# Index scores and the search for the 256th score moved ahead of the other input projections

## The chip, the cores and the metric

The kernel runs on one core of one Trainium2 chip. The metric is the device time of one execution in microseconds (us). Five engines work side by side: PE (TensorE, matrix products; PEld is its weight load), DVE (VectorE), ACT (ScalarE), POOL (GpSimd) and SP, which issues the transfers (DMA). Each runs its own list of instructions in order, and they wait for each other by semaphores.

## What is computed

Two layers of a decoder for a prompt of 1024 rows and a sample group of 8 x 4 rows that has 4096 cached rows each. Only the attention of layer 0 for the prompt matters here; the rest (sample attention, feed-forward layers, an RWKV-7 layer) is not edited.

```
proj = h @ w_in      # qa ka va | qb kb vb | qi ki wi  (stick-breaking | sparse | index)
oa = stick_breaking(qa, ka, va)                  # 8 heads
score = sum_h wi[h] * relu(qi[h] . ki) / sqrt(64 * 8)   # index score of every key for every query
sel = top_k(score with later keys at -inf, 256)
ob = softmax attention of qb over kb, vb, over the keys in sel only
```

qb, kb, qi and ki are turned by rotary tables (cos, sin) of their positions. The value of the 256th largest score of each query is found by a search over the bits of a float: for each of 31 bits, count the scores that are at least a candidate, and keep the bit if there are 256 or more.

## The kernel before

All rows (1024 + 32 = T = 1056) are kept transposed: features on the 128 partitions, rows along the free dimension. The stages are separated by barriers of all engines (the class Stage, its exit). Those up to the end of the prompt's attention, in order:

- `stage_enter` (L144) loads x, normalises it and transposes it to xT (in oT) and hT; SP also loads the first two weight tiles (`follow`, L174) and the page numbers, and at the end saves xT to memory (`K.x_save`).
- `stage_project` (L241) makes 24 output tiles, 12 rounds of two, of 128 features x 1056 rows each: 24 products of 128 x 128 by 352 columns per tile (L310), into two banks `acc[0]` and `acc[1]` in turn. DVE evacuates each tile: plainly in one operation (qa, ka, va, vb: L335, L337; wi: L339), or with rotary in six (qb, kb, qi, ki: L342, four of L345, L348). PE begins a tile when the bank's last content has been evacuated (semaphore `taken`) and its weights are there; SP loads weights of a tile when the product two tiles earlier is done. The rotary tables and a scratch tile lie in oT, and are loaded by SP once xT is saved. The order of the rounds is qa/ka, va/qb, vb/kb, qi/qi, ki/wi.
- `stage_rows` (L355) transposes ka, va, kb, vb, ki and wi (L372 to L378) to rows, writes the outputs, and keeps vtok (values by row) and wtok (index weights, scaled, L395).
- `stage_index_prompt` (L427): for each of the 6 query tiles that have more than 256 keys, and each of 8 index heads, PE makes the products (L445), ACT takes the relu (L456), DVE weighs and adds (L465, L468). The scores stay in `A.scores`.
- `stage_stick_prompt` (L544): 48 steps (4 head pairs, 2 query chunks of 512, 4 or 8 key tiles). Per step and two heads: PE scores (L576), ACT exp (L633), DVE cap (L654), ACT log (L635), DVE maximum (L664) and, on diagonal tiles, mask (L669), PE suffix products (L584, and L589 with the running sum that DVE makes, L682), ACT exp (L627), DVE mask on diagonal tiles (L650), PE output (L606). The score banks are three, `z[0..2]`; PE issues the suffix of step m - 2, the output of m - 3 and the scores of m in one turn. Between these, DVE carries out the search (`Threshold`, L476): 288 operations, spread evenly over the turns by the line quoted below. One operation is a count over one query tile (L500, with an accumulator read of its own), or one of three small ones per bit (L524, L532, L535).
- `stage_sparse_prompt` (L691) uses scores and thresholds for the masked softmax attention.

```
goal = Threshold.OPS * (2 * m + 1) // (2 * M + 6)
while asked < goal:
    search.advance(dve, A, asked)
    asked += 1
```

Of the kernel before, what the change touches and what calls it, by code (L numbers as in the profile page):

```python
# [21 lines left out]
P = 128  # L22
# [81 lines left out]
def row3(ap):  # L104

    return ap.rearrange("p (c n) -> p c n", c=NCH)
# [134 lines left out]
def stage_project(nc, K, w_in, hT, A, free, w):  # L241

    W = w_in[0].rearrange("(k p) n -> p k n", p=P)
    with Stage(nc, "proj") as s:
        s.sems.append(K.saved)
        cos, sin, half = (free[:, i, :] for i in range(3))
        acc = [s.ps(f"acc{u}", [P, NCH, 512]) for u in range(2)]
        w_loaded = [s.sem(f"w_loaded{u}") for u in range(2)]
        tables, product, taken, steps = s.sem("tables"), s.sem("product"), s.sem("taken"), s.sem("steps")
        block = s.block()  # L250

        DHS = bass.ds

        def pair_src(i, base):
            return [(W[:, :, DHS(i * P + base, P)], slice(0, P))]

        def qb_src(i):
            return [(W[:, :, DHS(i * DH + OFF_QB, DH)], slice(0, DH)),
                    (W[:, :, DHS(i * DH + OFF_QB + HP * DH, DH)], slice(DH, P))]

        ki = [(W[:, :, OFF_KI:OFF_KI + DH], slice(0, DH)), (W[:, :, OFF_KI:OFF_KI + DH], slice(DH, P))]
        wi = [(W[:, :, OFF_WI:OFF_WI + 8], slice(0, 8))]
        rounds = [
            (4, lambda i: pair_src(i, 0), "query", lambda i: A.qa[:, DHS(i, 1), :],
             lambda i: pair_src(i, OFF_KA), "copy", lambda i: A.ka[:, DHS(i, 1), :]),
            (4, lambda i: pair_src(i, OFF_VA), "copy", lambda i: A.va[:, DHS(i, 1), :],
             qb_src, "rope", lambda i: A.qb[:, DHS(i, 1), :]),
            (1, lambda i: pair_src(0, OFF_VB), "copy", lambda i: A.vb[:, :, :],
             lambda i: pair_src(0, OFF_KB), "rope", lambda i: A.kb[:, :, :]),
            (2, lambda i: pair_src(2 * i, OFF_QI), "rope", lambda i: A.qi[:, DHS(2 * i, 1), :],  # L270
             lambda i: pair_src(2 * i + 1, OFF_QI), "rope", lambda i: A.qi[:, DHS(2 * i + 1, 1), :]),
            (1, lambda i: ki, "rope", lambda i: A.ki[:, :, :],
             lambda i: wi, "weights", lambda i: A.wi[:, :]),
        ]
        n_loads = [[len(r[1 + 3 * u](0)) for u in range(2)] for r in rounds]

        @block.sync
        def _(sp):
            sp.sem_inc(w_loaded[0], 16)
            sp.sem_inc(w_loaded[1], 16)  # L280
            with sp.Fori(0, rounds[0][0] - 1) as i:
                for u in range(2):
                    sp.wait_ge(product, 2 * i + u + 3)
                    for src, cols in rounds[0][1 + 3 * u](i + 1):
                        sp.dma_start(w[u][:, :, cols], src).then_inc(w_loaded[u], 16)
            sp.wait_ge(K.saved, 16)
            sp.dma_start(cos[:, :], K.cos).then_inc(tables, 16)
            sp.dma_start(sin[:, :], K.sin).then_inc(tables, 16)
            done = rounds[0][0]
            for n, r in enumerate(rounds[1:]):  # L290
                with sp.Fori(0, r[0]) as i:
# [4 lines left out]
                done += r[0]  # L296

        @block.tensor
        def _(pe):
            pe.sem_inc(product, 2)  # L300
            done, loads = 0, [0, 0]
            for n, r in enumerate(rounds):
                with pe.Fori(0, r[0]) as i:
                    for u in range(2):
                        pe.wait_ge(w_loaded[u], 16 * (i * n_loads[n][u] + n_loads[n][u] + loads[u]))
                        pe.wait_ge(taken, 2 * i + 2 * done + u + 1)
# [7 lines left out]
                loads = [loads[u] + r[0] * n_loads[n][u] for u in range(2)]  # L314

        @block.vector
        def _(dve):
            dve.sem_inc(taken, 2)  # L318
            link = Link(dve, steps)
            done = 0  # L320
            for n, r in enumerate(rounds):
                if n == 1:
                    dve.wait_ge(tables, 32)
                per = sum({"rope": 2}.get(r[2 + 3 * u], 0) for u in range(2))
                with dve.Fori(0, r[0]) as i:
                    if per:
                        link.enter(i, per)
                    for u in range(2):
                        kind, dst = r[2 + 3 * u], r[3 + 3 * u](i)
                        dve.wait_ge(product, 2 * i + 2 * done + u + 3)  # L330
# [9 lines left out]
                        else:  # L340
# [9 lines left out]
                if per:  # L350
                    link.leave(r[0], per)
                done += r[0]


def stage_rows(nc, K, A, O):  # L355


    with Stage(nc, "rows") as s:
# [6 lines left out]
        def _(pe):  # L365
            for t in range(NT + 1):
# [10 lines left out]
                pe.transpose(tp[t % 2][0:n, 2, 2 * P:2 * P + DH], A.ki[0:DH, 0, cols], K.ident[0:DH, 0:DH])  # L377
                pe.transpose(tp[t % 2][0:n, 2, 320:328], A.wi[:, cols], K.ident[0:8, 0:8]).then_inc(turned, 1)  # L378

        @block.vector  # L380
        def _(dve):
            for t in range(NT + 1):
# [6 lines left out]
                dve.tensor_copy(row[t % 2][0:n, 2, 0:328], tp[t % 2][0:n, 2, 0:328]).then_inc(taken, 1)  # L389
                dve.wait_ge(taken, 3 * t + 3)  # L390
                if t < NT:
                    dve.tensor_copy(A.vtok[:, t, 0:512], row[t % 2][:, 1, :])
                    dve.tensor_copy(A.vtok[:, t, 512:640], row[t % 2][:, 2, P:2 * P])
# [33 lines left out]
def stage_index_prompt(nc, K, A):  # L427

    units = [(qt, h) for qt in CHOOSING for h in range(8)]
    with Stage(nc, "index") as s:  # L430
        kept = [s.sb(f"kept{i}", [P, SEQ]) for i in range(3)]
        prod = [s.ps(f"prod{i}", [P, 1024]) for i in range(3)]
        product, relued, weighed = s.sem("product"), s.sem("relued"), s.sem("weighed")
        block = s.block()

        @block.tensor
        def _(pe):
            for u, (qt, h) in enumerate(units):
                if u >= 3:
                    pe.wait_ge(relued, u - 2)  # L440
                rows = slice((h % 2) * DH, (h % 2) * DH + DH)
# [17 lines left out]
        def _(dve):  # L459
            for u, (qt, h) in enumerate(units):  # L460
# [15 lines left out]
class Threshold:  # L476
# [5 lines left out]
    def __init__(self, s):  # L482
        self.n = len(CHOOSING)
        self.found, self.flip, self.cand, self.more = (s.sb(x, [P, self.n], I32) for x in ("found", "flip", "cand", "more"))
        self.count = s.sb("count", [P, self.n])
        self.junk = s.sb("junk", [P, sum((qt + 1) * P for qt in CHOOSING)], BF16)
# [57 lines left out]
def stage_stick_prompt(nc, K, A, oT):  # L544
# [12 lines left out]
    with Stage(nc, "stick") as s:  # L557
        expd, soft, wgt = (s.sb(x, [P, R, 2, 512]) for x in ("expd", "softplus", "weight"))
        later = s.sb("later", [P, 2, 2, 512])
        search = Threshold(s)  # L560
# [82 lines left out]
        def _(dve):  # L643
            asked = 0
            for m in range(M + 3):
# [2789 lines left out]
```

## Time and profile before

| | us |
|---|---|
| time, median of 3 executions (lowest to highest) | 5399.53 (5394.25 to 5403.45) |
| time of the profiled execution | 5401.57 |
| its span, first to last instruction | 5399.8 |
| PE busy | 4599.8 (85%) |
| DVE busy | 2292.2 (42%) |
| ACT busy | 1088.0 (20%) |
| POOL busy | 350.0 (6%) |
| mean granted clock of PE, as a share of full speed | 0.914 |

Busy time is the union of an engine's recorded instructions. PE's products are pipelined and their ends are modelled, so a busy PE need not be one at its peak. The granted clock is 1.00 at 2.4 GHz and 0.50 at 1.2 GHz; a mean in between is a mix of the two. In lists of instructions a row has start, duration, engine, line, operation, tiles, shapes, how many were merged, and in brackets the idle time of the engine in front of it with what ended it. In groups a row has the engine, line and shapes, how many, then the busy time in us and the mean in ns of one, then the idle time before them.

### The profile page before, as it was taken

To read this page: it belongs to the slowest core of one execution; us is meant where nothing else is said; L and a number is where in the kernel's file an instruction comes from. 1 tells how busy PE (TensorE), PEld (TensorE's weight loads), DVE (VectorE), ACT (ScalarE), POOL (GpSimd) and SP (SyncE) were. 2 spreads that over 40 slices of the span, in tenths; PEclk is the share of its full clock that TensorE was granted. 3 is DMA by queue.
4 is the path that set the end of the run, shared out by engine and by line. 5 is a ranking of instruction groups with operands and counts; after the bars stand their busy time and mean duration, and the time that the engine had idled before them with its cause. 6 is when DMAs were issued, how large, how long until landed. Compare 5 with 4: busy or idle time off the path is not lost. (4 is left out here: it accounts for less than half of the span.)

```text
span 5399.8 us, 75557 instructions
## 1 busy us (share of the span) xinstructions
PE 4599.8 (85%) x30371; PEld 2899.1 (54%) x30371; DVE 2292.2 (42%) x3248; ACT 1088.0 (20%) x1971; POOL 350.0 (6%) x523
## 2 busy tenths in 40 slices
PE   8997777777767799999996999577777879999997
PEld 5663223344434466665663645376765546666564
DVE  1248997369921323232004122487685242323102
ACT  1004333344431122221000010222122022222000
POOL 0000000410063000000000000111110000000000
PEclk9998987889978899999997989788888889999998
DMA  2110000289964011111101221412213201111111
GB/s 92 47 39 27 1 0 1 52 288 352 357 181 139 24 35 39 35 39 47 33 22 58 71 82 61 164 30 53 57 30 142 63 24 39 35 39 46 35 33 43
DMA packets 434190, 398.60 MB, mean 74 GB/s; under 512 B 71613, under 2 KB 351717, under 8 KB 429494
## 3 DMA queue, kind: packets, MB, share of 16 engines
q1 hardware_dynamic: 419042, 347.23, 20.2%
q0 software_dynamic: 12288, 21.00, 1.4%
q10 hardware_dynamic: 2584, 26.50, 1.3%
q8 instruction: 197, 3.23, 0.3%
q14 instruction: 79, 0.65, 0.0%
HBM read 341.43 MB, written 53.06 MB: 73 GB/s over the span
## 5 line engine op out<-in xcount | busy, mean ns | idle before, releaser
L2086 PE MATMUL fup_acc<-h,w_up_first 128*128 128x352 f32 x2112 | 636.8, 462 | 28.1 <-ACTq L2093 28.1
L2086 PE MATMUL fup_acc<-h,fup_w 128*128 128x352 f32 x2112 | 632.0, 459 | 0.0
L2086 PEld LDWEIGHTS fup_acc<-h,w_up_first 128*128 128x128 f32 x2112 | 403.5, 191 | 255.4 <-ACTq L2093 30.2
L2086 PEld LDWEIGHTS fup_acc<-h,fup_w 128*128 128x128 f32 x2112 | 401.3, 190 | 223.5
L2129 DVE TENSOR_SCALAR fup_c<-fup_u,taps 128x1072 f32<-128x1072 f32 x88 | 73.7, 838 | 852.1 <-ACT last_u L2106 852.1
L310 PE MATMUL proj_acc<-hT,w_in 128*128 128x352 f32 (+1 forms) x1152 | 344.0, 462 | 1.8 <-DVEq L318 1.8
L1970 PE MATMUL fdown_acc<-hidden,w_down_first 128*128 128x352 f32 x1056 | 317.4, 463 | 0.0
L1970 PE MATMUL fdown_acc<-hidden,fdown_w 128*128 128x352 f32 x1056 | 314.5, 460 | 2.4 <-DVE h L1889 2.4
L310 PEld LDWEIGHTS proj_acc<-hT,w_in 128*128 128x128 f32 (+1 forms) x1152 | 215.4, 187 | 129.9 <-issue 12.4
L1970 PEld LDWEIGHTS fdown_acc<-hidden,w_down_first 128*128 128x128 f32 x1056 | 202.1, 192 | 115.7 <-issue 6.5
L2099 ACT ACTIVATE fup_u<-fup_acc 128x704 f32<-128x704 f32 x88 | 66.7, 757 | 974.6 <-PE fup_acc L2086 974.6
L1970 PEld LDWEIGHTS fdown_acc<-hidden,fdown_w 128*128 128x128 f32 x1056 | 200.0, 190 | 116.5 <-issue 3.4
L2016 DVE COPY h<-fdown_acc 128x1056 f32<-128x1056 f32 x16 | 20.1, 1255 | 541.0 <-PE fdown_acc L1970 541.0
L500 DVE TENSOR_SCALAR_CACHE_REDUCE stick_junk<-scores,stick_cand 128x384 bf16<-128x384 f32 (+1 forms) x186 | 167.2, 941 | 0.7
L2624 POOL TENSOR_TENSOR scan_om<-scan_low,scan_level 128x512 f32<-128x512 f32 x80 | 122.8, 1546 | 508.4 <-PE scan_u L2706 389.3
L584 PE MATMUL stick_z<-stick_softplus,tri 128*128 128x512 f32 (+3 forms) x192 | 93.3, 617 | 65.6 <-DVE stick_softplus L669 44.5
L1995 ACT ACTIVATE fdown_square<-h 128x1056 f32<-128x1056 f32 x16 | 17.3, 1083 | 652.1 <-DVE h L2016 652.1
L1190 DVE MAX8 sstick_best<-vtok 32x8 f32<-32x4100 f32 x32 | 141.1, 4409 | 0.0
L1193 DVE MATCH_REPLACE8 vtok<-sstick_best,vtok 32x4100 f32<-32x4100 f32 x32 | 140.8, 4401 | 0.0
L2706 PE MATMUL scan_u<-scan_Tm,scan_om 64*64 64x64 f32 x2560 | 95.4, 234 | 42.8 <-DVE scan_TT L3031 35.4
L2713 PE MATMUL scan_u<-scan_X,scan_TT 64*64 64x64 f32 x2048 | 86.6, 242 | 49.7 <-ACT scan_X L2902 43.7
L1103 ACT ACTIVATE sstick_kT<-sstick_tp 128x512 f32<-128x512 f32 x248 | 127.8, 596 | 2.4 <-PE sstick_tp L996 2.3
(582 smaller groups left out, 6846.5 us busy)
## 6 DMA issues: line engine op xcount, KB each, us to landing
sstick_own<-in_cache_sb_k SPq DMA_DIRECT2D x128, 256.0 KB, 5.8
qb<-in_cache_sb_k SPq DMA_DIRECT2D x128, 256.0 KB, 6.2
qi<-in_cache_sb_v SPq DMA_DIRECT2D x128, 256.0 KB, 5.8
ka<-in_cache_sb_v SPq DMA_DIRECT2D x128, 256.0 KB, 6.2
w_up_first<-in_ffn_w_up SPq DMA_DIRECT2D x44, 512.0 KB, 3.7
fup_w<-in_ffn_w_up SPq DMA_DIRECT2D x44, 512.0 KB, 3.8
w_down_first<-in_ffn_w_down SPq DMA_DIRECT2D x8, 1408.0 KB, 7.0
fdown_w<-in_ffn_w_down SPq DMA_DIRECT2D x8, 1408.0 KB, 7.0
```

The costliest lines, as they stand in the source:

```text
L310: last = pe.matmul(acc[u][0:m, c, 0:CW], w[u][:, k, 0:m], hT[:, k, c * CW:(c + 1) * CW], start=(k == 0), stop=(k == KD - 1))
L500: self.mark(dve.tensor_scalar(self.junk[:, at:at + (CHOOSING[t] + 1) * P], score, at_least, 0.0, ALU.is_ge, ALU.add, accum_out=self.count[ ...
L584: last = pe.matmul(z[m % R][:, par, c:512], K.tri[:, :], soft[:, m % R, par, c:512], start=False, stop=True, skip_group_check=True)
L1103: act.activation(kT[:, p % 2, :, i % 4, (i // 4) * P:(i // 4 + 1) * P], tp[t % 3][:, :].rearrange("p (f n) -> p f n", f=HP), ACT.Copy).the ...
L1190: link(dve.max(best[:, :], score))
L1193: link(dve.match_replace(score, best[:, :], score, LOW))
L1970: last = pe.matmul(acc[n % 2][:, c, 0:CW], w[n % 2][:, k, :], src[:, k, c * CW:(c + 1) * CW], start=(k == 0), stop=(k == kt - 1))
L2086: last = pe.matmul(acc[u][:, c, 0:CW], w[u][:, k, :], hT[:, k, c * CW:(c + 1) * CW], start=(k == 0), stop=(k == KD - 1))
L2129: link(dve.tensor_scalar(c, ubuf[u][:, 0:CO], tap[0], tap[3], ALU.mult, ALU.add))
L2624: pool.tensor_tensor(om[:, heads(g), :], low2[:, heads(g), 0, :], level[:, l, :].unsqueeze(1).to_broadcast(full), ALU.mult).then_inc(om_re ...
L2706: last = pe.matmul(spot(h, c, False), om[half(c), h, :], Tm[half(c), h, :], start=True, stop=True, skip_group_check=True)
L2713: last = pe.matmul(spot(h, c, False), TT[half(c), h, :], X[half(c), h, :], start=True, stop=True, skip_group_check=True)
```

## The change

The 24 tiles are projected in two stages: first the six of the index (qi, ki, wi), then the other 18. The index stage runs between the two. The search is taken out of `stage_stick_prompt` and put into the second projection stage, where DVE does a share of it after each evacuation, by weights of 2 for a rotary tile and 4 for another. The index stage transposes wi itself, in place of `stage_rows`, and SP loads the first two weight tiles of the other projections there. The rotary tables are loaded in `stage_enter`, into vtok. Loops of `stage_project` are written out. Scratch tiles are laid into tensors that are idle at the time, and `A.scores` lives until the end of the attention, where two tiles of the sample stages are laid into it.

```diff
+def input_rounds(W, A):
...
+    index = [
+        (2, lambda i: pair_src(2 * i, OFF_QI), "rope", lambda i: A.qi[:, DHS(2 * i, 1), :],
+         lambda i: pair_src(2 * i + 1, OFF_QI), "rope", lambda i: A.qi[:, DHS(2 * i + 1, 1), :]),
+        (1, lambda i: ki, "rope", lambda i: A.ki[:, :, :],
+         lambda i: wi, "weights", lambda i: A.wi[:, :]),
+    ]
+    others = [
+        (4, lambda i: pair_src(i, 0), "query", lambda i: A.qa[:, DHS(i, 1), :],
+         lambda i: pair_src(i, OFF_KA), "copy", lambda i: A.ka[:, DHS(i, 1), :]),
+        (4, lambda i: pair_src(i, OFF_VA), "copy", lambda i: A.va[:, DHS(i, 1), :],
+         qb_src, "rope", lambda i: A.qb[:, DHS(i, 1), :]),
+        (1, lambda i: pair_src(0, OFF_VB), "copy", lambda i: A.vb[:, :, :],
+         lambda i: pair_src(0, OFF_KB), "rope", lambda i: A.kb[:, :, :]),
+    ]
+    return index, others
...
+def stage_project(nc, K, name, rounds, hT, A, w, done_too=None, junk=None):
...
+        cos, sin, half = K.tables
...
+        search = Threshold(s, junk) if junk is not None else None
...
         def _(sp):
...
+                for i in range(1 if n == 0 else 0, r[0]):
                     for u in range(2):
-                        sp.wait_ge(product, 2 * i + 2 * done + u + 1)
+                        sp.wait_ge(product, 2 * (done + i) + u - 1)
                         for src, cols in r[1 + 3 * u](i):
                             sp.dma_start(w[u][:, :, cols], src).then_inc(w_loaded[u], 16)
                 done += r[0]
+            if done_too is not None:
+                sp.wait_ge(done_too, 16)
...
         def _(dve):
...
+            kinds = [r[2 + 3 * u] for r in rounds for i in range(r[0]) for u in range(2)]
+            room = [2 if kind == "rope" else 4 for kind in kinds]
...
                             link(last)
+                            dve.sem_inc(taken, 1)
                             link(dve.tensor_tensor(dst, dst, row3(half[:, :]), ALU.add))
-                            dve.sem_inc(taken, 1)
...
+                        if search:
+                            goal = Threshold.OPS * sum(room[:at + 1]) // sum(room)
+                            while asked < goal:
+                                search.advance(dve, A, asked)
+                                asked += 1
                 done += r[0]
+            if search:
+                assert asked == Threshold.OPS
+                search.finish(dve, A.least[:, :])
...
-                pe.transpose(tp[t % 2][0:n, 2, 320:328], A.wi[:, cols], K.ident[0:8, 0:8]).then_inc(turned, 1)
...
-                dve.tensor_scalar(A.wtok[0:n, t, :], row[t % 2][0:n, 2, 320:328], (DH * 8) ** -0.5, None,
-                                  ALU.mult).then_inc(stepped, 1)
...
+def stage_index_prompt(nc, K, A, free, follow):
...
+        def _(sp):
+            for dst_w, dram in follow:
+                sp.dma_start(dst_w, dram).then_inc(followed, 16)
+            sp.wait_ge(followed, 16 * len(follow))
...
         def _(pe):
+            for t in range(NT + 1):
+                n = P if t < NT else NS
+                last = pe.transpose(prod[2][0:n, t * 8:t * 8 + 8], A.wi[:, t * P:t * P + n], K.ident[0:8, 0:8])
+            last.then_inc(turned, 1)
...
         def _(dve):
+            dve.wait_ge(turned, 1)
+            for n, ts in ((P, slice(0, NT)), (NS, slice(NT, NT + 1))):
+                dve.tensor_scalar(A.wtok[0:n, ts, :], prod[2][0:n, 0:8 * NT + 8].rearrange("p (t h) -> p t h", h=8)[:, ts, :],
+                                  (DH * 8) ** -0.5, None, ALU.mult).then_inc(laid, 1)
+            dve.wait_ge(laid, 2)
...
-                goal = Threshold.OPS * (2 * m + 1) // (2 * M + 6)
-                while asked < goal:
-                    search.advance(dve, A, asked)
-                    asked += 1
...
-                goal = Threshold.OPS * (2 * m + 2) // (2 * M + 6)
-                while asked < goal:
-                    search.advance(dve, A, asked)
-                    asked += 1
-            assert asked == Threshold.OPS
-            search.finish(dve, A.least[:, :])
...
                     stage_enter(nc, K, I.x_prompt, I.x_sample, I.page_table, I.norm_mix_pre[0], oT, hT, A,
-                                [(w[0][:, :, :], W[:, :, 0:P]), (w[1][:, :, :], W[:, :, OFF_KA:OFF_KA + P])])
-                    stage_project(nc, K, I.att_w_in, hT, A, oT, w)
+                                [(w[0], W[:, :, OFF_QI:OFF_QI + P]), (w[1], W[:, :, OFF_QI + P:OFF_QI + 2 * P]),
+                                 (K.tables[0], K.cos), (K.tables[1], K.sin)])
+                    stage_project(nc, K, "proji", index, hT, A, w, done_too=K.saved)
+                    stage_index_prompt(nc, K, A, free, [(w_later[0], W[:, :, 0:P]), (w_later[1], W[:, :, OFF_KA:OFF_KA + P])])
+                    stage_project(nc, K, "proj", others, hT, A, w_later, junk=oT[:, 0:2, :].rearrange("p k t -> p (k t)").bitcast(BF16)[:, 0:A.scores.shape[1]])
                 stage_rows(nc, K, A, O)
```

## Rows read from the trace of the kernel before

**Rows 1.** Stretches of time: projection, rows, index, stick-breaking. Stretch: length, busy by engine, clock, DMA, GB/s
```profile
46.60:391.90 345.30, 344.04 (x1152) 215.43 (x1152) 92.88 (x74) 0.00 (x0) 0.00 (x0) 0.99 0.15 40
391.90:423.30 31.40, 19.81 (x108) 15.81 (x108) 20.46 (x53) 0.00 (x0) 0.00 (x0) 0.69 0.54 181
423.30:475.60 52.30, 46.68 (x160) 24.18 (x160) 44.78 (x54) 35.99 (x48) 0.00 (x0) 0.92 0.00 1
475.60:806.00 330.40, 243.90 (x746) 98.62 (x746) 308.42 (x706) 121.83 (x154) 0.00 (x0) 0.89 0.00 1
```

**Rows 2.** Groups of instructions of the search, first 1000 us
```profile
L500 DVE TENSOR_SCALAR_CACHE_REDUCE stick_junk<-scores,stick_cand 128x384 bf16<-128x384 f32 (+1 forms) x186 | 167.2, 941 | 0.7
...
L500 DVE DVE_READ_ACCUMULATOR stick_junk<-scores,stick_cand 128x1 f32 x186 | 15.4, 83 | 0.0
...
L524 DVE SCALAR_TENSOR_TENSOR stick_cand<-stick_found,stick_flip 128x6 int32<-128x6 int32 x31 | 5.0, 163 | 0.7
```

**Rows 3.** Waits of the stick-breaking stage: total us, times, longest
```profile
ACT stick_expd L635 <- DVE stick_expd L654: 159.9, 48, 5.7
...
PE stick_z L584 <- DVE stick_softplus L669: 44.5, 27, 3.1
```

**Rows 4.** Order of time, stick-breaking stage: PE's products of steps with 512 columns
```profile
657.28 1.98 PE L584 MATMUL stick_z<-stick_softplus,tri 128*128 128x512 f32 x4 [1.91 <-DVE stick_softplus L669]
...
659.10 1.88 PE L589 MATMUL stick_z<-stick_later,negones 128*128 128x512 f32 x4
...
664.50 1.08 PE L606 MATMUL stick_o<-stick_weight,vtok 128*64 128x512 f32 x4 [0.52 <-DVE stick_weight L650]
...
672.61 1.13 PE L576 MATMUL stick_z<-qa,ka 64*128 64x512 f32 x4
```

**Rows 5.** Order of time, same stage: DVE and ACT in a step of 384 columns
```profile
671.77 0.42 DVE L650 TENSOR_TENSOR stick_weight<-stick_weight,bound 128x256 f32<-128x256 f32 x1
...
672.70 0.93 ACT L635 ACTIVATE stick_expd<-stick_expd,one 128x768 f32<-128x768 f32 x1 [5.41 <-DVE stick_expd L654]
...
673.66 0.95 DVE L664 TENSOR_TENSOR stick_softplus<-stick_expd,stick_z 128x768 f32<-128x768 f32 x1 [0.52 <-ACT stick_expd L635]
...
675.27 0.89 DVE L682 TENSOR_TENSOR stick_later<-stick_softplus,stick_later 128x768 f32<-128x768 f32 x1
```

**Rows 6.** Stretches of 2 us around the same step
```profile
670.00:672.00 2.00, 0.11 (x1) 0.00 (x0) 2.00 (x5) 0.00 (x0) 0.00 (x0) 1.00 0.00 0
...
676.00:678.00 2.00, 2.00 (x5) 1.09 (x4) 2.00 (x6) 0.00 (x0) 0.00 (x0) 0.50 0.00 0
```

**Rows 7.** The projection's tile: ns least/median/most of one, first and last start, forms
```profile
L310 PE MATMUL proj_acc<-hT,w_in x1152: 459/459/951, 46.6 to 390.2; 128*128 128x352 f32 x184, 128*8 128x352 f32 x8
L345 DVE TENSOR_TENSOR oT<-proj_acc,oT x40: 1246/1252/1262, 193.1 to 381.4; 32x1056 f32<-32x1056 f32 x40
L335 DVE TENSOR_SCALAR qa<-proj_acc x4: 1258/1258/1258, 64.1 to 149.3; 128x1056 f32 x4
L337 DVE COPY ka<-proj_acc x4: 1258/1258/1258, 78.3 to 163.5; 128x1056 f32 x4
...
L339 DVE COPY wi<-proj_acc x1: 1245/1245/1245, 390.7 to 390.7; 8x1056 f32<-8x1056 f32 x1
```

**Rows 8.** Order of time, stick-breaking stage: a count of the search and what follows
```profile
598.15 1.27 DVE L500 TENSOR_SCALAR_CACHE_REDUCE stick_junk<-scores,stick_cand 128x1024 bf16<-128x1024 f32 x1
599.35 0.08 DVE L500 DVE_READ_ACCUMULATOR stick_junk<-scores,stick_cand 128x1 f32 x1
599.47 0.17 DVE L532 TENSOR_SCALAR stick_more<-stick_count 128x6 int32<-128x6 f32 x1
```

**Rows 9.** Groups of the rows stage; last, a transfer: KB, us to landing
```profile
L378 PE MATMUL rows_tp<-ident,wi 8*128 8x8 f32 (+1 forms) x9 | 2.2, 239 | 0.0
...
L395 DVE TENSOR_SCALAR wtok<-rows_row 128x8 f32<-128x8 f32 (+1 forms) x9 | 1.5, 164 | 0.0
...
x_save<-oT SPq DMA_DIRECT2D x1, 4224.0 KB, 11.4
```

More of the change, by code:

```diff
@@ L238, in _, with pair_src, qb_src @@
             take(NT)
[L241 to L246, printed above, removed]
+def input_rounds(W, A):
+    DHS = bass.ds
+    def pair_src(i, base):
+        return [(W[:, :, DHS(i * P + base, P)], slice(0, P))]
+    def qb_src(i):
+        return [(W[:, :, DHS(i * DH + OFF_QB, DH)], slice(0, DH)),
+                (W[:, :, DHS(i * DH + OFF_QB + HP * DH, DH)], slice(DH, P))]
+    ki = [(W[:, :, OFF_KI:OFF_KI + DH], slice(0, DH)), (W[:, :, OFF_KI:OFF_KI + DH], slice(DH, P))]
+    wi = [(W[:, :, OFF_WI:OFF_WI + 8], slice(0, 8))]
+    index = [
[13 more added lines that the diff above has]
+    return index, others
@@ L250, in stage_project @@
         block = s.block()
[L252 to L274, printed above, removed]
@@ L280, in _ @@
             sp.sem_inc(w_loaded[1], 16)
[L281 to L291, printed above, removed]
+            done = 0
+            for n, r in enumerate(rounds):
+                for i in range(1 if n == 0 else 0, r[0]):
                     for u in range(2):
-                        sp.wait_ge(product, 2 * i + 2 * done + u + 1)
+                        sp.wait_ge(product, 2 * (done + i) + u - 1)
                         for src, cols in r[1 + 3 * u](i):
@@ L296, in _ @@
                 done += r[0]
+            if done_too is not None:
+                sp.wait_ge(done_too, 16)
         @block.tensor
         def _(pe):
-            pe.sem_inc(product, 2)
             done, loads = 0, [0, 0]
             for n, r in enumerate(rounds):
-                with pe.Fori(0, r[0]) as i:
+                for i in range(r[0]):
                     for u in range(2):
-                        pe.wait_ge(w_loaded[u], 16 * (i * n_loads[n][u] + n_loads[n][u] + loads[u]))
-                        pe.wait_ge(taken, 2 * i + 2 * done + u + 1)
+                        loads[u] += n_loads[n][u]
+                        pe.wait_ge(w_loaded[u], 16 * loads[u])
+                        if done + i >= 1:
+                            pe.wait_ge(taken, 2 * (done + i) + u - 1)
                         m = 8 if r[2 + 3 * u] == "weights" else P
@@ L313, in _ @@
                 done += r[0]
-                loads = [loads[u] + r[0] * n_loads[n][u] for u in range(2)]
         @block.vector
         def _(dve):
-            dve.sem_inc(taken, 2)
             link = Link(dve, steps)
-            done = 0
+            kinds = [r[2 + 3 * u] for r in rounds for i in range(r[0]) for u in range(2)]
+            room = [2 if kind == "rope" else 4 for kind in kinds]
+            asked = done = 0
             for n, r in enumerate(rounds):
[L322 to L327, printed above, removed]
+                for i in range(r[0]):
                     for u in range(2):
+                        at = 2 * (done + i) + u
                         kind, dst = r[2 + 3 * u], r[3 + 3 * u](i)
-                        dve.wait_ge(product, 2 * i + 2 * done + u + 3)
+                        dve.wait_ge(product, at + 1)
                         if kind != "weights":
@@ L3347, in build @@
             A.vtok = sb(att, "vtok", [P, NT, 640])
+            A.scores = sb(att, "scores", [P, sum((qt + 1) * P for qt in CHOOSING)])
+            spare = A.vtok[:, :, :].rearrange("p t n -> p (t n)")
+            K.tables = [spare[:, i * T:(i + 1) * T] for i in range(3)]
             with ExitStack() as c:
```

43 lines of the change are left out of this document (22 added, 21 removed).

## Prediction

> **What bounds the kernel now.** I read the busy time of each engine stage by stage first, then the groups of instructions of the stage that has the search, then its waits, and at last single steps in order of time. The stages are separated by barriers, so what an edit is worth is read stage by stage. In the table of stages the reader is to see which engine is full in each [rows 1]: the input projections keep TensorE (PE) at 344.0 of 345.3 us with VectorE (DVE) at 92.9; in the index stage DVE, at 44.8 of 52.3, sets the pace, with ACT close; in the stick-breaking stage DVE is busy for 308.4 of 330.4 us while PE has 243.9 and a granted clock of 0.89. So the search sits in the one stage of this stretch in which DVE is already the bound, and DVE idles for 250 us in a stage that PE bounds.
>
> The groups say how much of the 308 us is the search [rows 2]: 186 counting passes of 167.2 us, their 186 accumulator reads of 15.4, and three small instructions per bit, 31 of each, of which one group has 5.0. With the other two small groups at the same 0.16 us and the six counts of the sign pass (6 x about 0.95) it is 167 + 15 + 15 + 6 = 204 us as recorded. DVE's own work for attention is the rest, about 105 us net of overlap. The waits show who pays [rows 3]: ACT's logarithm waits for DVE's cap 48 times, 159.9 us in all, and PE's suffix product waits another 44.5 us for DVE.
>
> **The change, part by part.**
>
> *The search leaves the stick-breaking stage.* What ends last there afterwards? PE per full step (512 columns, no half clock): the two products of the suffix, 1.82 us from start to start and 1.88, the output 1.08 and the scores 1.13 [rows 4]; end to end that is 5.9, and since the last two overlap their successors I take 5.6. There are 24 such steps of 48. A narrow diagonal step is bounded by the round between DVE and ACT instead: mask of the weights at 671.77, cap, logarithm at 672.70, maximum at 673.66, mask, the sum from 675.27 for 0.89 [rows 5]; what the search has in between lies under the logarithm, so a step of 384 columns costs 4.3 to 4.4. Four of the operations in this round scale with the width, each by 0.25 to 0.3 us per 128 columns (0.89 for three such blocks of two heads), so about 1 us less for each block: 3.4 at 256 columns, 2.5 at 128 (estimates), 8 steps each. Sum: 24 x 5.6 + 8 x (4.35 + 3.4 + 2.5) = 134 + 82 = 216. The first step has to pass through the round before PE has a second product, and the last one through the round, the suffix and the output; I put 10 for both: 226 at full clock. The clock takes some of it: after 2 us with PE at 0.11 busy it stands at 0.50 (1.2 GHz) while PE is at 2.00 of 2.00 [rows 6]. A mean of 0.89 is 22% of the stage at half clock; those gaps of PE come in part from DVE's lateness, which goes, and in part from the narrow steps, which stay. Keeping all 22% with PE always the bound would give 226 / 0.89 = 254; I take 240. The stage falls from 330 to 240: **-90 us**; the bounds are -104 (full clock) and -65 (265: 254 and 11 us of waits that I cannot see here).
>
> *The search goes between the evacuations of 18 projected tiles.* A tile of 128 columns is ready every 14.2 us (four evacuations of qa from 64.1 to 149.3, two tiles each) [rows 7]. DVE's room: the change deals 288 operations out by weights, 4 for a plain evacuation and 2 for a rotary one, 62 in all, so 18.6 or 9.3 operations per tile. A bit is nine operations. From one count's start to the next is its length less 0.07 (598.15 to 599.35 for the recorded 1.27) [rows 8], so the six counts of a bit take 167.2 / 31 - 6 x 0.07 = 5.0, the last read and the three small ones with their waits about 0.9: 5.9 us, 0.65 per operation, some 189 us in all. A plain tile needs 1.26 + 12.2 = 13.4 us, a rotary tile 1.26 + 4 x 1.25 + 1.26 + 6.1 = 13.6 [rows 7]. Both are under 14.2, the evacuation comes before the search, and PE needs a bank only one tile later: PE does not wait, and 17 of the 18 shares cost nothing, covered by PE's 14.2 us a tile. If the cover fails, each us that DVE needs above 14.2 costs up to 18. The last tile's share has no cover: rotary evacuation 7.5 + 10 operations 6.5 + the finish 0.3 = 14.3 us after PE's last product, where before one evacuation of 1.25 stood [rows 7]: **+13**.
>
> The recorded lengths and the spacing of counts speak differently here. The Trainium skill ("VectorE: DVE Perf Modes", The DRAIN you can't avoid) says that the next operation cannot issue until the pipe of the one in front is empty. Laid end to end by that rule, the search is 204 us, a plain tile 14.4, and the sum would be some 5 us later; the rows, where the next count starts before the recorded end of the one in front, speak for the spacing.
>
> *Two projection stages in place of one, with the index stage between.* The first tile of a stage costs 17.5 us from PE's start at 46.6 to 64.1, not 14.2, since PE starts at half clock [rows 7, 6]; PE is idle for some 5 us at the end of the index stage, so this is paid twice: **+3**. One barrier more: **+1** (bounds 0.7, the step from DVE's last index operation into the next stage, to 2). SP's queue: the two tables go ahead of the page numbers and the saving of x in the loading stage, and nobody there waits for either; the save lands 11.4 us after its issue [rows 9], inside the 89 us of the six index tiles, so SP's new wait at their end is over long before. The two first weight loads of the other projections are issued at the start of the index stage, where SP has nothing else: no cost. The later weight loads keep their one-tile lead.
>
> *Index weights turned in the index stage.* Nine transposes of about 0.24 us and nine scalings of 0.16 [rows 9] leave the rows stage (**-1**); the same transposes and two scalings precede the index products (+2, of which about 1 comes back because PE is no longer at half clock there): **+1**. Loops written out, buffers laid into other tensors, the sample stages' new places: 0, bounds -2 to +2; PE's loop cost shows in no row (1.8 us idle in the whole stage).
>
> **The sum.** -90 + 13 + 3 + 1 - 1 + 1 = **-73 us** against the profiled execution's 5401.6 us (span 5399.8): 5328.6. That execution lies 2.0 above the median of the runs shown, 5399.5, so I say 5327. Nothing downstream moves: the sparse stage needs scores and thresholds, which are both there earlier.
>
> **Rivals.**
> (a) *Another wait takes the place of DVE's.* Stick-breaking stays a chain over three engines with three banks; if each step still ends with PE waiting for the round of rows 5, full steps too, the stage would come to 285 or more: a full step is then 4.4 x 1024/768 + two masks, about 6.7, and the clock stays at 0.89: (24 x 6.7 + 82 + 10) / 0.89 = 284. Gain of 46 instead of 90: 5371. For it: the two-step lead of the suffix leaves under 1 us of slack in a full step by my count. Against it: full steps off the diagonal have no mask, and their work on DVE is three operations, a little over 3 us of 5.6.
> (b) *The search is not hidden.* DVE at 14.4 or more per tile makes it the bound: at the recorded lengths +5, with 0.3 us more for each count 192 x 0.3 = 58 us, less the 14 us of slack that 18 tiles hold: +44. That gives 5332 to 5371. For it: only 0.6 to 0.8 us are free per tile. Against it: the same counts were measured beside a busy PE in the stick-breaking stage.
> (c) *PE's clock collapses in the stick-breaking stage, and the kernel gets slower.* The mechanism is that of rows 6: a PE that pauses at the narrow steps falls to 1.2 GHz, and the PE-bound steps that now set the time run at that speed. At half clock throughout, a full step is 11.2, a 384-column step 7.7, then 5.1 and 2.6: 24 x 11.2 + 8 x 15.4 + 20 = 412 us, 82 more than now: 5499. It decides once the stage exceeds 313 us, that is when some 174 of them are at half clock (mean 0.72). The stage has 0.89 with more pauses than it will have; the rows stage, at 0.69, shows such a mean is possible [rows 1]. The Trainium skill ("TensorE: Matmul & The Clock Gate", HAM oscillation) describes this: pauses between bursts send the engine back to the lower clock again and again. The trace agrees on the fall, not on its lasting.
>
> **How the numbers follow.** Forecast 80%, its own range 5305 to 5358: -104 + 18 less 8 for index, rows and barriers at their lower ends, to -65 with +24. (a) 10%, (b) 7%, (c) 3%. The range 5305 to 5362 holds most of the forecast (0.72) and the lower half of (b) and a little of (a): 0.8. A measurement of this kernel cannot tell less than about 0.2% (11 us) from no change. Faster: forecast, (a) and nearly all of (b), 95%; same: what is left of (b), 2%; slower: (c), 3%.
>
> **What would show it.** In the changed profile: no count under the stick-breaking stage, which should last 226 to 265 us with PE rather than DVE the fullest engine, and ACT's 159.9 us of waiting for the cap down to a third; evacuations in the second projection stage still 14.2 us apart; 12 to 16 us between PE's last projection product and the rows stage; the index stage within 2 us of 52.3. Wrong would be: tile spacing above 14.5 (then b), full steps at 6.5 or more with PE waiting for DVE or ACT (a), a granted clock under 0.75 in the stage (c).

## The result, and the profile after

The changed kernel took 5314.37 us (median of 4 executions, 5305.44 to 5318.03), the kernel before beside it 5400.68 (4 executions, 5394.25 to 5403.45): a ratio of 0.9839, 95% interval 0.9822 to 0.9856, or 86 us less. The forecast was 73 less. The profiled execution took 5318.03 us with a span of 5316.4.

The stages first, with the columns of [rows 1]: the stretch and its length, busy time by engine, the granted clock, the DMA share and GB/s. In order they are the index projection, the index stage, the second projection with the search, the rows stage and stick-breaking. The last line is a small stage late in the kernel, needed only at the end.

```profile
46.10:135.90 89.80, 88.19 (x288) 51.13 (x288) 38.90 (x31) 0.00 (x0) 0.00 (x0) 0.97 0.14 42
135.90:189.30 53.40, 47.07 (x169) 25.27 (x169) 45.07 (x56) 35.87 (x48) 0.00 (x0) 0.89 0.08 20
189.30:462.70 273.40, 258.37 (x864) 165.43 (x864) 238.72 (x524) 0.00 (x0) 0.00 (x0) 0.97 0.12 31
462.70:492.00 29.30, 18.25 (x99) 14.86 (x99) 19.68 (x43) 0.00 (x0) 0.00 (x0) 0.73 0.58 195
492.00:724.00 232.00, 215.52 (x744) 88.48 (x744) 133.29 (x224) 125.29 (x153) 0.00 (x0) 0.98 0.00 1
...
3055.00:3091.00 36.00, 31.50 (x104) 16.65 (x104) 14.37 (x26) 12.69 (x11) 0.00 (x0) 0.95 0.32 132
```

Against [rows 1]: projection 345.3 to 89.8 + 273.4, which is 17.9 more; index 1.1 more; rows 2.1 less; stick-breaking 330.4 to 232.0, 98.4 less. Together that is 81.5 less. The sparse stage begins its first product at 724.3 in place of 805.9, 81.6 earlier. From there to the end it is 4592.1 us, 4593.9 before. DVE's busy time says what moved: 308.4 to 133.3 in stick-breaking, while the second projection has 238.7. PE, with 215.5 of 232.0, is now the fullest engine of stick-breaking, and its idle time there is 16.5 us, 86.5 before.

The waits of the stick-breaking stage (engine, line and the engine waited for; us in total, times, the longest):

```profile
DVE stick_softplus L675 <- ACT stick_expd L651: 48.1, 48, 1.2
ACT stick_expd L651 <- DVE stick_expd L669: 46.1, 48, 1.6
...
PE stick_z L600 <- DVE stick_softplus L680: 14.6, 23, 1.8
```

The second line answers to the 159.9 us of [rows 3], the third to the 44.5. ACT waited 3.3 us for each cap, because DVE was in a count when the exponential was done; now it is 1.0.

The evacuations of the second projection (ns least/median/most of one, first and last start, forms):

```profile
L334 DVE TENSOR_SCALAR qa<-proj_acc x4: 1258/1258/1258, 206.7 to 291.9; 128x1056 f32<-128x1056 f32 x4
...
L341 DVE TENSOR_TENSOR kb<-proj_acc,vtok x1: 1258/1258/1258, 448.1 to 448.1; 128x1056 f32<-128x1056 f32 x1
```

The first tile's evacuation starts at 206.7 and the eighteenth's at 448.1, and 206.7 + 17 x 14.2 = 448.1: no tile is late. What DVE waits for PE's products in this stage,

```profile
DVE qa L334 <- PE proj_acc L313: 19.7, 4, 17.7
...
DVE ka L336 <- PE proj_acc L313: 4.3, 4, 1.7
```

with four smaller lines for the other tiles, is 29.0 us in all. Less the 17.7 for the first tile, that is 11.3 over 17 tiles: 0.7 us of room per tile, and the forecast had 0.6 to 0.8. No line has PE waiting for DVE. The end of the stage in order of time (start, duration, engine, line, operation, tiles, shapes, how many):

```profile
448.14 1.26 DVE L341 TENSOR_TENSOR kb<-proj_acc,vtok 128x1056 f32<-128x1056 f32 x1 [1.21 <-PE proj_acc L313]
...
455.91 0.17 DVE L552 TENSOR_TENSOR proj_found<-proj_found,proj_more 128x6 int32<-128x6 int32 x1
...
462.04 0.17 DVE L556 TENSOR_TENSOR least<-proj_found,proj_flip 128x6 int32<-128x6 int32 x1
463.16 1.09 PE L377 MATMUL rows_tp<-ident,ka 128*128 128x128 f32 x4 [15.05 <-PEq L95]
```

This is the cost of the new place: the rotary evacuation until 455.9, then ten operations of the search and its finish until 462.2, which no product covers, and PE idle for 15.05 us.

### The profile page after: what moved, and what is told of

It reads as the page before. It is cut to its first block and busy times, and to the rows that moved or that the text cites. A ratio compares the mean times of both kernels' runs of the same rounds, so it can differ in the third digit from the quotient of the medians.

```text
span 5316.4 us, 75362 instructions
## 1 busy us (share of the span) xinstructions
PE 4564.2 (86%) x30371; PEld 2890.8 (54%) x30371; DVE 2301.2 (43%) x3241; ACT 1093.0 (21%) x1971; POOL 351.0 (7%) x523
## 5 line engine op out<-in xcount | busy, mean ns | idle before, releaser
L313 PE MATMUL proj_acc<-hT,oT 128*128 128x352 f32 x864 | 258.4, 462 | 6.2 <-SPq L287 6.2
L313 PEld LDWEIGHTS proj_acc<-hT,oT 128*128 128x128 f32 x864 | 165.4, 192 | 99.4 <-SPq L287 7.1
L517 DVE TENSOR_SCALAR_CACHE_REDUCE oT<-scores,proj_cand 128x384 bf16<-128x384 f32 (+1 forms) x186 | 164.4, 942 | 1.1
L2135 DVE SCALAR_TENSOR_TENSOR fup_c<-fup_u,taps,fup_c 128x1072 f32<-128x1072 f32 x88 | 117.4, 1335 | 12.8 <-DVE fup_c L2134 0.3
```

The source lines that it names most:

```text
L313: last = pe.matmul(acc[u][0:m, c, 0:CW], w[u][:, k, 0:m], hT[:, k, c * CW:(c + 1) * CW], start=(k == 0), stop=(k == KD - 1))
L517: self.mark(dve.tensor_scalar(self.junk[:, at:at + (CHOOSING[t] + 1) * P], score, at_least, 0.0, ALU.is_ge, ALU.add, accum_out=self.count[ ...
L2135: link(dve.scalar_tensor_tensor(out=c, in0=ubuf[u][:, 1:1 + CO], scalar=tap[1], in1=c, op0=ALU.mult, op1=ALU.add))
```

## The experiments

Theory: the search cost its time because it stood in a stage bound by DVE's rounds, and costs nothing beside PE's tiles, the last tile excepted. Rivals: the new order of the stages brings the gain by itself; or the search still costs time where it is now; or the number of DVE's operations matters and not their place. An execution's time from the sparse stage on varies (last section), so the stage lengths and the place of the sparse stage's first product (724.3 and, again, 723.3 for the changed kernel) are read beside the times. Diffs are against the changed kernel, unless said otherwise.

**The search put back between the stick-breaking steps, in the new order of the stages.**

```diff
+                goal = Threshold.OPS * (2 * m + 1) // (2 * M + 6)
+                while asked < goal:
+                    search.advance(dve, A, asked)
+                    asked += 1
...
-                    stage_project(nc, K, "proj", others, hT, A, w_later, junk=...)
+                    stage_project(nc, K, "proj", others, hT, A, w_later)
```

> The new order of the stages is kept, the search goes back between the steps of stick-breaking. Theory (the gain is the search's place, the new order only costs): stick-breaking back at 325 to 335 us with DVE at about 308 and a clock near 0.89, the second projection stage 7.5 us of rotary evacuation after PE's last product instead of 14; the kernel 5 to 12 us slower than before (one more start at half clock 3, one more barrier 1, the tail 6). Rival (the new order itself brings part of the gain, by the clock or the earlier weight loads): 20 us or more faster than before with the search back in its old place.

5428.83 us (10 executions), ratio to the kernel before 1.0047 (1.0031 to 1.0063). Second projection and stick-breaking, columns as above, then the wait for the cap:

```profile
189.30:456.00 266.70, 258.12 (x864) 165.31 (x864) 54.02 (x43) 0.00 (x0) 0.00 (x0) 0.98 0.12 32
486.00:815.00 329.00, 248.68 (x736) 101.43 (x744) 308.71 (x705) 122.45 (x153) 0.00 (x0) 0.86 0.00 0
```

```profile
ACT stick_expd L652 <- DVE stick_expd L671: 153.3, 48, 5.7
```

With the search the 308.7 us of DVE, the 329 us of the stage and the 153 us of waits are all back. The sparse stage begins at 815.3, 9.4 later than before: that is what the new order costs, together with the small edits that came with it, so it brings nothing by itself. The median is 30 above that of the kernel before beside it (5398.55), where 5 to 12 had been expected and the stages account for 9.4; the last group of experiments comes back to this.

**The search left out.**

```diff
+            dve.memset(A.least[:, :], 0.0)
...
-                    stage_project(nc, K, "proj", others, hT, A, w_later, junk=...)
+                    stage_project(nc, K, "proj", others, hT, A, w_later)
```

> The search is left out; the thresholds are set to 0. Theory (the search is hidden under PE but for the share of the last tile): the projection stage shorter by 6.5 to 8 us, all of it after PE's last product, stick-breaking unchanged at 232, the kernel 5 to 10 us faster than the changed one (5304 to 5310). Rival (the counts slow PE or the evacuations): the spacing of the tiles falls below what the changed kernel shows and the kernel is 20 us or more faster than the changed one.

5318.14 us, ratio 0.9841 (0.981 to 0.9872). Second projection and stick-breaking:

```profile
188.40:455.10 266.70, 258.31 (x864) 165.38 (x864) 54.04 (x44) 0.00 (x0) 0.00 (x0) 0.98 0.12 32
484.50:716.00 231.50, 214.06 (x736) 88.29 (x744) 133.28 (x224) 125.19 (x153) 0.00 (x0) 0.98 0.00 1
```

184.7 us of DVE's work gone (238.7 less 54.0) shorten the stage by 6.7: that is the uncovered share of the last tile, and all that the search still costs in this stage. The sparse stage begins at 716.3, 7 to 8 earlier. The time expected, 5304 to 5310, did not come: the gain is lost in what executions differ by.

**The widest count made twice per bit**, to see where the cover ends.

```diff
+            if at == self.n:
+                self.mark(dve.tensor_scalar(self.junk2, index_scores(A, CHOOSING[at - 1]), self.cand[:, at - 1:at].bitcast(F32), 0.0,
+                                            ALU.is_ge, ALU.add, accum_out=self.again[:, :]))
```

> The count over the 1024 scores is made twice for each of the 31 bits: 31 x 1.2 = 37 us more on DVE in the second projection stage. Theory (DVE has 11 us left in the stage, its waits for PE after the first tile): the stage grows by 37 - 11 = 26 us (22 to 30) and DVE's waits for PE vanish; kernel 5336 to 5344. Rival 1 (DVE has much room): 0 to 8 us. Rival 2 (DVE is the bound already): 35 to 40.

5365.46 us (10 executions), ratio 0.9939 (0.9917 to 0.996). The stage, then a wait that the changed kernel does not have:

```profile
190.90:490.40 299.50, 264.03 (x864) 167.50 (x864) 274.86 (x586) 0.00 (x0) 0.00 (x0) 0.94 0.11 29
```

```profile
PE proj_acc L315 <- DVEq L349: 9.9, 4, 5.1
```

36.1 us more on DVE, less the 11.3 of room, are 24.8; the stage grew by 26.1, and PE now waits until a bank is evacuated, and for 25.64 us in place of 15.05 at the end of the stage. The search fitted by 0.7 us per tile, and rival (b) was that close. The sparse stage begins at 751.5, 27 later than in the changed kernel; the median lies 51 above it, where 5336 to 5344 had been expected, and no stage before the sparse one holds the rest.

**Equal shares**, 16 operations after each tile, rotary or not.

```diff
-            room = [2 if kind == "rope" else 4 for kind in kinds]
+            room = [1 for kind in kinds]
```

> The changed kernel with the search dealt out in equal shares, 16 operations per tile, in place of 18.6 beside a plain and 9.3 beside a rotary evacuation. A plain tile then takes DVE 11.7 us and a rotary one 18.0, above the 14.2 of PE. Theory (DVE falls behind at each rotary tile and what it is late by shows after PE's last product): 2 to 3 us late and a longer last share, the projection stage 280 us (278 to 283) in place of 273. Rival (only the sum over the stage counts): 273 within 1.

5330.18 us (one execution). The stage:

```profile
188.70:472.90 284.20, 258.27 (x864) 165.30 (x864) 238.37 (x524) 0.00 (x0) 0.00 (x0) 0.95 0.12 30
```

10.8 us longer with the same work, a little more than the 278 to 283 expected. The evacuation of kb, the last tile, starts at 453.40, which is 5.9 later than in the changed kernel if counted from the stage's first product, and PE is then idle for 26.04 us, not 15.05. The weights of 2 and 4 are what keeps rotary tiles on time.

**A plain tile last, with no share.** The last round projects kb before vb, and vb's tile gets no search.

```diff
+            room[-1] = 0
```

> The last two tiles change places, so that a plain evacuation is last, and the last tile gets no share of the search; the other 17 get it all. Theory (the 14 us after PE's last product are the last tile's own evacuation and share): 1.3 us of evacuation and what DVE is late by then, 1 to 4 us, are left; the kernel 9 to 12 us faster than the changed one. Rival (DVE has no room for it in the 17 tiles): the same work ends later inside the stage, the gain is under 5 us.

5324.64 us (5293.34 to 5354.58), ratio 0.9862 (0.9801 to 0.9924). The stage:

```profile
188.40:451.00 262.60, 258.39 (x864) 165.42 (x864) 237.56 (x524) 0.00 (x0) 0.00 (x0) 0.99 0.13 33
```

10.8 us shorter, as expected: the tail was the last tile's. The sparse stage begins at 712.9, 11.4 earlier, but the executions lie 61 us apart, and their time does not show a gain.

**The same, and 18 of the 288 operations left for stick-breaking, one per full-width step, right behind the cap.**

```diff
+LEFT = 18
...
+                    if c == 0 and asked < Threshold.OPS:
+                        search.advance(dve, A, asked)
+                        asked += 1
...
```

> As the run with a plain evacuation last and no share for the last tile, and besides the last 18 of the 288 operations of the search (two bits) are done in stick-breaking, one in each of the first 18 full steps, under the logarithm. Theory: DVE is no longer late at the end of the projections, the stage 260 to 262 us (13 under the changed kernel), stick-breaking 232 to 235, with one more barrier of 1 us: 9 to 13 us faster than the changed kernel beside it. Rival (an operation of the search in a step costs its length there): stick-breaking 245 or more, no gain over the changed kernel.

5319.21 us (5306.8 to 5341.5), ratio 0.9855 (0.9829 to 0.9881). Projection and stick-breaking:

```profile
188.40:449.30 260.90, 258.29 (x864) 165.60 (x864) 226.87 (x493) 0.00 (x0) 0.00 (x0) 0.99 0.13 33
479.20:711.00 231.80, 214.64 (x744) 87.99 (x744) 144.30 (x255) 125.22 (x153) 0.00 (x0) 0.98 0.00 1
```

11.0 us of DVE's work cost stick-breaking nothing there, and the sparse stage begins at 711.1. Still no gain in the median.

**A useless count of 1.2 us in each stick-breaking step, behind the cap or at the end of the step.** Two kernels with the same three lines at two places; the first stands between cap and maximum, while ACT makes the logarithm.

```diff
+                    if m >= 1:
+                        dve.wait_ge(dosed, m)
+                    dve.tensor_scalar(junk[:, :], index_scores(A, NT - 1), 0.0, 0.0, ALU.is_ge, ALU.add, accum_out=tally[:, :]).then_inc(dosed, 1)
```

> The changed kernel, and in each of the 48 steps of stick-breaking one count over 1024 scores of no use (1.2 us, 58 in all on DVE), placed between the cap and the maximum, where DVE waits for ACT's logarithm. Theory (the place in the round between DVE and ACT decides): free in full steps, where the logarithm takes 1.15 us, 0.3 to 0.7 us in each narrow one: the stage 232 + 12 (8 to 16). Rival (only the sum of DVE's work counts: 133 + 58 is still under PE's 215): 0 to 3.

> The same count, placed at the end of each step, behind the running sum. Theory: it lies in the round of the 24 narrow steps with its whole 1.2 us (29) and in part in the 8 full diagonal steps (6), and is free in the 16 full steps off the diagonal, which have over 1 us to spare: the stage 232 + 35 (28 to 42). Rival (only the sum counts): 0 to 3.

The stage with the count behind the cap (5338.36 us, one execution):

```profile
491.70:726.20 234.50, 215.41 (x744) 88.33 (x744) 185.66 (x320) 125.33 (x153) 0.00 (x0) 0.98 0.00 1
```

The stage with the count at the end of the step (5342.2, one execution):

```profile
493.00:748.50 255.50, 221.82 (x744) 90.26 (x744) 186.11 (x320) 122.05 (x153) 0.00 (x0) 0.96 0.00 1
```

The count is 58 us of DVE's work in both (58.2 and 58.0), DVE's busy time differs by 0.5 us, and the stage by 21: 2.5 us longer in the one, 23.5 in the other. Behind the cap the result misses the expected 8 to 16. In the changed kernel DVE's maximum waits there for the logarithm (in brackets the idle time, at 256, 384 and 512 columns):

```profile
572.30 0.69 DVE L675 TENSOR_TENSOR stick_softplus<-stick_expd,stick_z 128x512 f32<-128x512 f32 x1 [0.79 <-ACT stick_expd L651]
...
576.07 0.95 DVE L675 TENSOR_TENSOR stick_softplus<-stick_expd,stick_z 128x768 f32<-128x768 f32 x1 [1.00 <-ACT stick_expd L651]
...
580.71 1.22 DVE L675 TENSOR_TENSOR stick_softplus<-stick_expd,stick_z 128x1024 f32<-128x1024 f32 x1 [1.22 <-ACT stick_expd L651]
```

So nearly the whole count fits: with it the suffix of a 256-column step comes 0.26 us later behind that of the 128-column step (3.42 in place of 3.16), and those of wider steps by 0.05 at most. At the end of the step the expected 28 to 42 was too much as well: 23.5. ACT's wait for the cap, 46.1 us in the changed kernel, is 98.7 there:

```profile
ACT stick_expd L653 <- DVE stick_expd L671: 98.7, 48, 3.5
```

Place decides, not the amount.

**The scores issued ahead of the output on PE.**

```diff
+                if m < M:
+                    scores(m)
                 if m >= 3:
                     output(m - 3)
-                if m < M:
-                    scores(m)
```

> The changed kernel; in each turn of stick-breaking PE issues the scores of step m ahead of the output of step m - 3, so that the exponential of step m can begin 0.4 to 1 us earlier. Theory (in the narrow steps the round of cap, logarithm, maximum, masks and sum on DVE and ACT sets the pace, and in full steps PE's own work; the scores are there in time for both): the stage stays within 3 us of 232. Rival (the loop through PE, suffix, output, scores and then the round, sets the pace in the narrow steps): 24 narrow steps shorter by 0.2 to 0.5 us, the stage 220 to 227.

5312.76 us (5305.65 to 5319.76), ratio 0.9834 (0.9818 to 0.985). The stage:

```profile
488.50:716.00 227.50, 216.13 (x744) 88.42 (x744) 132.95 (x224) 122.87 (x153) 0.00 (x0) 0.98 0.00 1
```

My expectation failed: from the first product of stick-breaking to that of the sparse stage it is 226.8 us, 231.7 in the changed kernel. The rival had the size (220 to 227), but not where it comes from, since only one of the three narrow intervals shrinks:

```profile
565.76 0.71 PE L600 MATMUL stick_z<-stick_softplus,tri 128*128 128x128 f32 x4
...
568.40 1.13 PE L600 MATMUL stick_z<-stick_softplus,tri 128*128 128x256 f32 x4
...
572.45 1.56 PE L600 MATMUL stick_z<-stick_softplus,tri 128*128 128x384 f32 x4 [0.30 <-DVE stick_softplus L680]
```

The suffix of a 256-column step now follows that of the 128-column step after 2.50 to 2.65 us, in place of 3.16, in seven of the eight pairs (not in the first), and PE no longer waits for it. That is 4.1 of the 4.9; most of the rest lies in the first round of narrow steps. The two intervals behind it stay as in the changed kernel (3.96 to 4.05 and 4.91). So PE's own order set the first of the narrow steps, and the round over DVE and ACT the other two.

**The same kernels again, and the kernel before with 15 us of useless additions at the end of its index stage.** The last one's diff, against the kernel before:

```diff
+            for n in range(12):
+                dve.wait_ge(weighed, len(units) + n)
+                dve.tensor_tensor(kept[0][:, :], kept[1][:, :], kept[2][:, :], ALU.add).then_inc(weighed, 1)
```

> The changed kernel once more, beside those that follow. Theory (what differs between executions of one program lies behind the attention, where stages come out at one clock or the other): the stages up to the sparse attention within 2 us of the first profile (273 and 232 us), the time 5305 to 5325, ratio 0.982 to 0.987.

> The kernel before once more, for a second profile. Theory (the part of the kernel from the sparse attention on varies from one execution to the next, whichever program): the stages up to there as in the first profile within 2 us (stick-breaking 330), the rest between 4588 and 4611 us, the band of the programs run so far. Rival (the rest is fixed for this program): 4594 within 2.

> The kernel before, with 12 additions of no use by VectorE at the end of the index stage, about 15.5 us in which TensorE has nothing to do; everything behind begins that much later. Theory (a shift alone moves the later stages to the other clock or not by chance): the rest of the kernel in the band 4588 to 4611, spread of the times 20 us or more, median 5408 to 5430. Rival (the rest does not care when it begins): median 5414 to 5418, spread under 10.

The changed kernel again: 5319.91 us (5304.75 to 5333.76), ratio 0.9833 (0.9812 to 0.9855), second projection 273.5. The kernel before again: 5402.6, its sparse stage beginning at 806.4, the rest 4594.5. That is the rival's number: the two profiles of the kernel before agree from the sparse stage on, so they show no variation, though among its executions beside other experiments there are 5419 and 5425. Delayed: 5426.17 (5411.95 to 5442.17), ratio 1.0048 (1.0035 to 1.0062). Its additions, in order of time:

```profile
475.90 15.08 DVE L476 TENSOR_TENSOR index_kept<-index_kept 128x1024 f32<-128x1024 f32 x12
```

They put the sparse stage 11.8 us later, not 15: from its first product to that of the sparse stage, stick-breaking took 326.1 us, 329.7 and 329.8 in the two profiles of the kernel before. Yet the median stands 24 above the kernel before beside it (5402.07); it and the spread of 30 us are those expected, not the rival's. So a shift alone, with no step of any later stage edited, changes what later stages take, and the 30 us of the first experiment need no cause in the order of the stages itself. That they have none there is not shown.

## Why the prediction was right

The mechanism was the forecast's, and the size differs by the stick-breaking term. Two of the prediction's readings do not hold as put, and neither changes a term. PE is busy for 46.7 us of the index stage, more than DVE's 44.8 [rows 1], so busy time alone does not show that DVE sets the pace there; and PE's idle time in the whole projection stage is 1.3 us, not 1.8.

*The search leaves the stick-breaking stage*: forecast -90, measured -98.4. Two parts were mis-sized, in opposite directions, and that they cancel in part is luck. The products of PE in order of time, at the start of one round of narrow steps:

```profile
570.34 0.71 PE L600 MATMUL stick_z<-stick_softplus,tri 128*128 128x128 f32 x4
...
573.50 1.13 PE L600 MATMUL stick_z<-stick_softplus,tri 128*128 128x256 f32 x4 [0.60 <-DVE stick_softplus L680]
...
577.54 1.56 PE L600 MATMUL stick_z<-stick_softplus,tri 128*128 128x384 f32 x4 [0.40 <-DVE stick_softplus L680]
...
582.45 1.99 PE L600 MATMUL stick_z<-stick_softplus,tri 128*128 128x512 f32 x4 [0.42 <-DVE stick_softplus L680]
...
587.93 1.98 PE L600 MATMUL stick_z<-stick_softplus,tri 128*128 128x512 f32 x4
```

From start to start: 3.16, 4.04, 4.91, then 5.48. The forecast had 2.5, 3.4 and 4.35 for the three narrow steps. DVE's rounds were right where they can be read: from cap to cap it takes 3.43 us at 256 columns, 4.30 at 384 and 5.15 at 512. The error is mainly which interval they bound. The suffix of a step waits for that step's own round, so the interval behind the 256-column suffix goes with the round of 384 columns (4.04), and the next with that of 512 (4.91). The interval behind the 128-column suffix is 3.16 for another reason: PE issued an output ahead of the scores. With the scores first (the last experiment on stick-breaking) it is 2.50 to 2.65, and 2.5 had been forecast. Three narrow steps are 12.1 in place of 10.25, over eight rounds +15. Full-width steps are 5.06 to 5.70, on average 5.4 in place of 5.6, over 24 steps -5. A head pair takes 56.5 us, four of them 226, where the steps had been forecast at 216.

*The clock takes some of it*: forecast +14, from 226 to 240. This step failed. The granted clock is 0.98, and at 226 us of steps a stage of 232 leaves 6 for fill, drain and clock together, where 24 had been put (10 for fill and drain, 14 for the clock). The 0.89 of before belonged to the 86 us of pauses that DVE's lateness made, not to the narrow steps that stay. In the experiment that puts the search back, the clock is down again, at 0.86. How much of the 98 is waits and how much clock was not separated.

*The search between evacuations*: 17 of 18 shares free, as forecast, and 184.7 us of DVE's work where 189 had been worked out. The spacing of the counts was the right price, not their recorded length: by the rule of the Trainium skill ("VectorE: DVE Perf Modes", The DRAIN you can't avoid), as costed in the prediction, tiles would have been 14.4 us apart; they are 14.2. The same section adds that a next operation that is not held starts earlier, and the counts do: in the last share one count of 1.14 us starts at 459.25 and the next at 460.32, 0.07 before its recorded end.

*The last tile*: +13. Before, the rows stage's first product followed PE's last projection product by 2.0 us; now PE is idle for 15.05.

*First tile, barrier, index, rows*: projection, with the last tile's tail, is 17.9 longer, where 13 + 3 + 1 had been put; the index stage 1.1 (1), the rows stage -2.1 (-1).

The sum by place is -81.6, against -73; the medians give -86. The 5 us between lie within what executions differ by from the sparse stage on.

Rival (a) did not occur: PE's waits for the round fell from 44.5 to 14.6 us, with none on full steps off the diagonal. Rival (b) begins some 10 us of DVE's work further on: of 36.1 us added there, 26.1 were paid. Rival (c): its rule (the Trainium skill, "TensorE: Matmul & The Clock Gate", HAM oscillation) ties the lower clock to pauses between bursts, and the trace agrees; but the pauses went with the search, so the clock rose from 0.89 to 0.98 and the rival's condition did not arise.

## What to carry to other kernels

Before moving work to a fuller use of an engine, find the stage in which that engine is not the bound, and compare the work with the room of one unit there (here 14.2 us a tile, 13.5 used on average): below it the work is free, above it nearly every microsecond is paid. Inside a round that passes over several engines, put extra work where its engine waits for another one's answer: 58 us of counts cost 2.5 us there and 23.5 at the end of the round. Where work is dealt out over units, the last unit has no cover, so give it the smallest share.

## What had not been expected

Executions of one program differ in later stages that nothing here edits. The same stage as in the last line of the first table, in the second profile of the changed kernel:

```profile
3060.50:3106.50 46.00, 41.25 (x104) 21.49 (x104) 14.13 (x26) 12.74 (x11) 0.00 (x0) 0.73 0.25 103
```

36.0 us at a granted clock of 0.95 in one execution, 46.0 at 0.73 in the other, with the same 104 products. From its first product with weights to the next stage's it took 34.8 to 35.0 us in four of the fourteen profiles taken (the changed kernel's first, plain tile last, 18 operations left over, scores first) and 45.2 to 45.7 in the other ten, those of the kernel before among them. The Trainium skill ("TensorE: Matmul & The Clock Gate", What's actually happening) says that the number of products at the lower clock varies from run to run; this agrees. The sparse stage, too, took 212 to 221 us in these profiles. Edits of 5 to 12 us, which the stage lengths show plainly, therefore vanish in the median: plain tile last, 18 operations left over and scores first reach the sparse stage 10, 12 and 7 us sooner than the changed kernel did in its second profile (723.3), and none is shown to be faster as a whole. Which later stages make the delayed kernel's slower executions longer stays open: its profiled execution was the fastest of its six.
